# Opening of a one-core hybrid-attention step: modulation blocks of 2, 2, 2, 2, 4, 4 feature tiles, product ranges of 2, 2, 2, 2, 8 steps, later tokens ahead of the modulation products

## What is computed

```
shift, scale, gate = split(silu(cond) @ w_ada + b_ada, 3)      # cond: c_ctx for the context, c for the latents
h = rms_norm(x, g_norm) * (1 + scale) + shift                  # 640 x 2048
z = h @ w_in                                                   # 2048 x 6656
... differential attention and grouped-query attention on z ...
x = x + gate * (mixed heads @ w_out);  y = rms_norm(x, g_final)
```

## Time and profile before

| | |
|---|---|
| median of 3 runs | 1256.2 us (1255.31 to 1256.62) |
| profiled execution | 1258.17 us, span of its instructions 1256.5 us |
| PE busy | 1224.9 us (97%) |
| DVE busy | 800.4 us (64%) |
| ACT busy | 619.0 us (49%) |
| mean granted clock of PE | 0.995 |
| HBM read | 144.18 MB |

### The profile page before, as it was taken

One profiled execution on the slowest core, in us unless ns is written; L12 is line 12 of the kernel. 1 busy time (PEld: TensorE's weight loads), 2 busy tenths in 40 slices (PEclk: granted clock), 3 DMA queues, 4 the chain that ended last, 5 costly groups with the idle time before them and its releaser, 6 DMA issues.

```text
span 1256.5 us, 16904 instructions
## 1 busy us (share of the span) xinstructions
PE 1224.9 (97%) x6251; PEld 991.2 (79%) x6251; DVE 800.4 (64%) x1242; ACT 619.0 (49%) x1296; POOL 258.1 (21%) x439
## 2 busy tenths in 40 slices
PE   5899999999999999999999999999999999999996
PEld 3455778888888888888888888888888888887885
DVE  4455488667586776755546374555647674788774
ACT  5422225545555465565556555555556666312223
POOL 1211033012031040222221221222223322210111
PEclk9999999999999999999999999999999999999998
DMA  9999242222221232312222131222224423656544
GB/s 352 371 379 340 84 110 76 56 74 77 76 94 46 67 105 54 98 59 82 69 63 86 51 91 51 82 59 83 59 72 134 141 81 102 250 177 230 188 135 176
DMA packets 130482, 156.45 MB, mean 125 GB/s; under 512 B 8304, under 2 KB 97040, under 8 KB 129632
## 3 DMA queue, kind: packets, MB, share of 16 engines
q1 hardware_dynamic: 116528, 109.60, 26.8%
q0 software_dynamic: 13424, 45.20, 11.6%
q10 hardware_dynamic: 448, 0.57, 0.1%
HBM read 144.18 MB, written 11.16 MB: 124 GB/s over the span
## 4 chain that ended last, share of the span: by engine, by line
PE 90%; DVE 3%; SPq 3%; DMA 2%; POOL 1%; ACT 1%; issue 0%; DVEq 0%; POOLq 0%; ACTq 0%
PE z_ps L704 24%; PE z_ps L706 23%; PE z_ps L705 23%; PE ring L795 5%; PE ring L884 4%; SPq L658 2%; PE ring L730 2%; PE ring L829 2%; PE ring L828 2%; PE ring L888 2%; DMA ada_raw<-in_w_ada_dram 1%; PE ring L705 1%; PE ring L706 1%; PE ring L891 1%; PE ring L704 1%; DMA gate_b<-gate_rows 0%
## 5 line engine op out<-in xcount | busy, mean ns | idle before, releaser
L704 PE MATMUL z_ps<-w_hi,xt_hi 128*128 128x512 f32 x1350 | 554.4, 411 | 3.3 <-DVE y_sb L1654 1.1
L706 PE MATMUL z_ps<-w_hi,xt_lo 128*128 128x512 f32 x1350 | 527.8, 391 | 0.0
L705 PE MATMUL z_ps<-w_lo,xt_hi 128*128 128x512 f32 x1350 | 527.1, 390 | 0.0
L1007 ACT ACTIVATE w_hi<-w_raw 128x512 fp32r<-128x512 f32 x270 | 169.3, 628 | 335.3 <-PE z_ps L706 306.9
L704 PEld LDWEIGHTS z_ps<-w_hi,xt_hi 128*128 128x128 f32 x1350 | 254.0, 188 | 69.4 <-issue 28.7
L1441 DVE TENSOR_TENSOR w_lo<-w_raw,w_hi 128x512 fp32r<-128x512 f32 x270 | 196.7, 732 | 161.7 <-ACT w_hi L1007 161.1
L706 PEld LDWEIGHTS z_ps<-w_hi,xt_lo 128*128 128x128 f32 x1350 | 253.4, 188 | 55.5
L705 PEld LDWEIGHTS z_ps<-w_lo,xt_hi 128*128 128x128 f32 x1350 | 254.8, 189 | 38.9
L1546 DVE TENSOR_REDUCE small<-s_sb 128x2 f32<-128x1536 f32 (+1 forms) x60 | 87.6, 1460 | 20.5 <-ACT s_sb L1007 20.5
L1153 ACT ACTIVATE s_sb<-s_sb,small 128x768 f32<-128x768 f32 (+1 forms) x120 | 97.9, 821 | 3.6 <-DVE small L1546 3.6
L1901 POOL TENSOR_TENSOR sg<-sg,zs 128x128 f32<-128x128 f32 (+1 forms) x60 | 38.0, 633 | 276.8 <-DVE sg L1511 276.2
(11 more groups left out here) (196 smaller groups left out, 1380.7 us busy)
## 6 DMA issues: line engine op xcount, KB each, us to landing
w_raw<-in_w_in_dram SPq DMA_DIRECT2D x188, 256.0 KB, 3.2
ada_raw<-in_w_ada_dram SPq DMA_DIRECT2D x64, 512.0 KB, 11.4
w_raw<-in_w_out_dram SPq DMA_DIRECT2D x64, 256.0 KB, 3.8
gate_raw<-in_w_ada_dram POOLq DMA_DIRECT2D x12, 1024.0 KB, 8.1
w_raw<-in_w_in_dram POOLq DMA_DIRECT2D x20, 256.0 KB, 6.3
o_spill<-row_st POOLq DMA_DIRECT2D x14, 320.0 KB, 3.8
row_st<-o_spill POOLq DMA_DIRECT2D x14, 320.0 KB, 3.2
x_sb<-in_x_sample_dram SPq DMA_DIRECT2D x4, 1024.0 KB, 9.2
```

What stands on the lines that cost most here:

```text
L704: pe.matmul(out, hi_l, hi_r, start=start, stop=False)
L705: pe.matmul(out, hi_l, lo_r, start=False, stop=False)
L706: return pe.matmul(out, lo_l, hi_r, start=False, stop=stop)
L1007: return act.activation(out, in_, ACT.Copy, **kw)
```

## The change

Three tables and two positions are changed; no arithmetic changes and no new function appears.

- Block 2 of 4 feature tiles becomes two blocks of 2; there are 6 blocks in place of 5. Loads 8 to 15 now have rows of 1 KB.
- The range (4, 8) becomes (4, 6) and (6, 8): q = 8, 9 KV; 10, 11 G; 12, 13 KV; 14, 15 G. Two more segments end in `z_add`.
- In the opening the products m4, m5 stand behind unit 11, m6 behind all transposes of the later tokens, m7 behind unit 17, block 1's columns behind unit 18, m8 and m9 behind unit 19. Before: m4 behind unit 5, m5 behind 9, m6 behind 11, m7 in the transposes, columns behind unit 13, m8 behind 15, m9 behind 18.
- The slots of blocks 2 to 5 are new. Block 2's columns stand behind unit 24 (q = 4, last tile), block 3's behind unit 45, block 4's behind 72, block 5's behind 96. Before: block 2's behind 36, block 3's behind 68, block 4's behind 93.
- POOL issues norms and rotary tables behind pair 10 in place of pair 5.

```diff
-ADA_TILES = [2, 2, 4, 4, 4]
+ADA_TILES = [2, 2, 2, 2, 4, 4]
...
-RANGES = [(0, 2), (2, 4), (4, SPLIT_K), (SPLIT_K, KT)]
+RANGES = [(0, 2), (2, 4), (4, 6), (6, SPLIT_K), (SPLIT_K, KT)]
...
-COPIED, ADDED, LAST_ADDED = (0, 1), (2, 3, 4, 5), (6, 7)
+COPIED, ADDED, LAST_ADDED = (0, 1), (2, 3, 4, 5, 6, 7), (8, 9)
...
-ADA_SLOTS = {2: [20, 22, 25, 29, 32, 35], 3: [38 + 4 * e for e in range(8)], 4: [70 + 3 * e for e in range(8)]}
-OPEN_ADA = {5: [(1, 0)], 9: [(1, 1)], 11: [(1, 2)], 15: [(2, 0)], 18: [(2, 1)]}
-OPEN_HT_ADA = {2: (1, 3)}
-OPEN_COLS = 13
+ADA_SLOTS = {2: [20, 23], 3: [28, 37, 40, 43], 4: [46, 49, 52, 56, 59, 63, 66, 70], 5: [73 + 3 * e for e in range(8)]}
+OPEN_ADA = {11: [(1, 0), (1, 1)], 17: [(1, 3)], 19: [(2, 0), (2, 1)]}
+OPEN_HT_ADA = {3: (1, 2)}
+OPEN_COLS = 18
...
-                if j == 5:
+                if j == 10:
```

## The result

The changed kernel takes 1259.9 us (median of 7 runs, 1259.3 to 1261.3) against 1256.2 us of the kernel before beside it (7 runs, 1255.1 to 1258.1). The ratio is 1.0031, 95% interval 1.0021 to 1.0041: slower by 3.7 us, above the forecast of 1256.8 and above its range. The profiled execution took 1260.35 us, its span is 1258.7 us.

A forecast was written before the change was run, and what follows sets the result against it. It took PE, busy 97% of the span, as the bound. Terms -4.97 + 2.1 + 0.65 + 1.3 - 0.88 + 0.85 + 1.5 = +0.55 us on the median 1256.2 gave 1256.8 us, range 1253.8 to 1258.8.

The forecast's parts named there:

- start of q = 4, opening's gain: In the reordered opening, other PE work covers the load waits; q = 4 starts at 54.05 us against 59.02, -4.97 us.
- waits before m10, m11: PE, now earlier, waits for loads 10 and 11, whose 1 KB rows come at 353 GB/s: +2.1 us together.
- q = 6: PE waits for segment 2's first DVE add, delayed by feature splits behind block 2's columns: +1.3 us.
- q = 8: The old PE wait goes, since segment 3's adds have nothing ahead of them on DVE: -0.88 us.
- q = 10: PE waits for a DVE add behind block 3's columns and both tile splits: +0.85 us.
- q = 20: PE waits for the last block's first feature tile, with three units left behind its columns instead of six: +1.5 us.
- The rule for the adds: DVE's first add at a segment's end comes C + 6.4 us with both tiles split, C being the columns' start.
- I add the sum to the median.: Final step: the +0.55 us sum goes on the median 1256.2, not the profiled 1258.17 us, giving 1256.75.
- Everything behind q = 24 is bound by PE and unchanged, so it shifts by the same amount.: Kernel behind q = 24: no new cost there; it only shifts by the sum, +0.55 us.
- Rival 1: Loads 10 and 11 are in time, their term falling to 0 to 0.3 us: 1254.8 us, chance 0.27.
- Rival 3: The 32 transposes in one piece, 36.7 to 44.0 us, run at half clock, 4 us more: 1260.8, chance 0.05.
- Rival 2: Half clock follows a new 1.3 to 1.8 us wait at m10, q = 6 or 20: 1258.5 us, chance 0.12.

The follow-up runs named there:

- after_again: The changed kernel, unchanged, run and profiled in another execution: 1258.5 us, ratio 1.0028 to the kernel before.
- tables_early: The changed kernel with norms and rotary tables issued behind pair 5 again: 1259.2 us, ratio 1.0028.
- tables_late: The kernel before with norms and rotary tables issued behind pair 10 and nothing else: 1255.1 us, ratio 1.0001.
- ranges_alone: The kernel before with only its third range cut into (4,6) and (6,8), ten segments; old blocks, slots and opening: 1261.9 us, ratio 1.0047.
- again: The kernel before, unchanged, profiled in another execution: 1254.8 us, ratio 0.9995.
- places3: The changed kernel with new slots for blocks 2 to 5, m7 and block 1's columns one unit earlier, tables behind pair 5, block 2's columns later: 1253.7 us.
- opening_alone: The kernel before with only the opening's order of the changed kernel: 1256.6 us, ratio 1.0008.
- blocks_alone: The changed kernel with the opening's order of the kernel before; blocks, ranges and slots new: 1260.1 us, ratio 1.0036.

## Why the prediction was wrong

**What held.** The sum of the mechanisms was +0.55 us for the way from the first product to the keys. By the earlier trace rows and the first transpose of the keys the profiled execution of before needed 145.7 us, so 146.2 was foretold; after needed 146.8 and after_again 146.6, on a stretch that holds no half clock. That the two ends lie within 0.6 us of each other is the mechanism in the main, and in part luck: an opening 0.9 us too fast stood against loads 0.7 us too slow. Term by term:

| step | foretold | measured |
|---|---|---|
| start of q = 4, opening's gain | 54.05, -4.97 | 55.41, -3.6; from the first product -4.1 |
| waits before m10, m11 | +2.1, together | +1.4 (0.23 and 1.19) |
| columns of the sixth block | +0.65 | not measured by itself; a set is 0.6 busy |
| q = 6 | +1.3 | +1.30 |
| q = 8 | -0.88 | no wait |
| q = 10 | +0.85 | +0.99 |
| q = 20 | +1.5 | +1.47 |
| norms and tables | 0 | 0 (tables_early, tables_late) |
| clock | 1.00 from 36 to 145 us | 1.00 |

The rule for the adds, from DVE's rows behind one set of columns, gave q = 6, as DVE's timeline of after shows:

```profile
64.20 0.16 DVE L1378 TENSOR_TENSOR mod_a<-mod_a,vec 128x4 f32<-128x4 f32 x1
...
68.02 0.83 DVE L1426 TENSOR_TENSOR xt_lo<-row_st,xt_hi 128x640 fp32r<-128x640 f32 x1
68.77 3.08 DVE L1451 TENSOR_TENSOR zs<-z_ps,zs 128x512 f32<-128x512 f32 x5
```

Columns at 63.03, both tiles split, and the first add ends by 69.5: C + 6.5. The prediction's own terms, 4.0 + 1.86 + 0.65, also make 6.5 and not the 6.4 that it wrote, and PE was there at C + 5.3 and not 5.1; the two slips cancel in the 1.3. ranges_alone extended the rule to a place that the change doesn't have, 3.43 us for 3.5.

**The steps that failed.** The 3.1 us between 1256.8 and 1259.9 come from two steps, by the reckoning below of about equal weight.

**First, the base: "I add the sum to the median."** The -4.97 us began from a q = 4 at 59.02 us, which holds the half clock of the earlier trace rows. again shows an execution without it that starts q = 4 at 57.70; from there the opening gains 2.6 us (29.2 less 26.6 us from the first product), not 4.1. The prediction saw that the profiled execution was 2.0 above the median, and still took the whole gain off the median. Either consistent way was open: the sum on the profiled time (1258.17 + 0.55 = 1258.7), or the sum without the half clock on the median (1256.2 + 0.55 + 1.6 = 1258.4). The second takes it that the median run had no half clock, which is inferred: of the four profiles with the old opening and the old blocks two have it (before, tables_late) and two have not (again, ranges_alone). Each run's mean granted clock is on record, but it does not sort them well: among 24 runs of before beside after_again, the 12 at 0.995 or 0.996 took 1255.9 us on average and the 12 at 0.997 or 0.998 took 1254.9, while the same two groups lie 0.2 us apart among the 29 beside places3. So the size of this step is good to about 1 us.

**Second, the stretch behind the change: "Everything behind q = 24 is bound by PE and unchanged, so it shifts by the same amount."** It is the step that put the wait for `k_lo` at nothing. The rest, some 1.5 us of 1259.9 less 1258.4, is of the size of this wait: 2.3 and 1.9 us in the two profiles of the changed kernel, 0.8 and none in the two of before. The 0.81 us at 178 us stood in the view of the earlier trace rows, which shows one of its two lines. The line held the warning: a wait that is there already has no cover, and each 0.1 us on the landing counts.

Between the two profiled executions themselves the times differ by 2.2 us, against 0.55 in the sum: 1.1 us between the milestones, 0.6 behind them and 0.5 ahead of the first product, where the change does nothing.

**The opening was 0.9 us too fast** (from the first product: 26.6 us to q = 4 in place of 25.7). 0.2 us of it is the wait before m5 (0.44, foretold 0.2), 0.2 the eight rounds of transposes (4.15 us for 3.95; six in 3.04 us would have made 4.05), and the rest lies in small gaps between the units 12 to 17 (4.7 us for 4.2) and at the start of q = 4 (0.80, foretold 0.2 to 0.6). **The loads were 0.7 us better** than taken. Their pace was the one chosen (348 to 352 GB/s in after, 353 in the working), and m11 found its load at 61.08 us where 60.3 was foretold; but PE came later still, at 56.3 to m10 where 54.75 was foretold.

**The rivals.** Rival 1 had the loads in time: they were not. Rival 3 was the nearest in time, 1260.8, but not by its mechanism: its 32 transposes in one piece ran from 39.62 to 43.77 us at full clock. Rival 2, 1258.5, fell too: waits of 1.30, 1.47 and 2.31 us were followed by no half clock in after. Its mechanism exists, though: opening_alone has it behind 2.79 us, ranges_alone behind 3.43.

The page of the Trainium skill (DMA: Bandwidth & Descriptors, Specifications) that would have had rows of 1 KB at line rate is not borne out here: blocks_alone and again differ by 9%. Where the rows were 2 KB under the same opening (opening_alone), there was no wait at m10 and m11.

## What to carry to other kernels

Before a gain is added to a median, see whether the profiled execution paid for it in the ordinary way: a second profile of the unchanged kernel costs little and separates what belongs to the kernel from what belongs to that execution. When a block's preparation and a segment's flush run on the same in-order engine, write down the distance in time of each flush from the last preparation ahead of it; here one such rule gave four waits to 0.15 us, one of them after the fact, and moving the preparations away from the flushes, with later places for two loads, took 5 us off the way to the keys. And look at every short wait behind the changed stretch, since it has no cover left.

## What the runs showed of the hardware

- The same idle time of PE has two outcomes. Behind 1.84 to 1.86 us before m7 the clock fell to 0.50 in two profiles (before, tables_late) and stayed at 1.00 in two (again, ranges_alone). It also stayed behind 2.53 us (blocks_alone, before m4), and it fell behind 2.79 (opening_alone) and 3.43 us (ranges_alone). The fall in before cost 1.6 us.
- Rows of 1 KB came at 348 to 355 GB/s, rows of 2 KB at 385 to 388, in stretches that were else alike.
- One packet of 16 KB in the queue that brings code took 0.9 to 1.4 us, and where it came while a transfer of 256 KB was under way, one of the transfer's 16 shares went on only when it had ended (ten of the 11 profiles with six blocks). The transfer landed after 4.6 to 5.6 us in these 11, and after 3.1 to 4.1 in the five with five blocks.
